# A mixer and a 32-expert layer on one core: 1536 weight columns pass through PSUM, and the loads of the second and third expert pair are cut anew

## Chip, cores, metric

One core of a Trainium2 chip. The metric is the time of one execution on the device in microseconds (us); lower is better.

## What is computed

One layer on 256 frames of width 1024, all in float32. Three mixers (retention, sliding-window attention, attention to a memory) share one input projection and one output projection; then comes a mixture of experts, 4 of 32 for each frame:

```python
h = rms_norm(x, g_mix[l])
proj = h @ w_in[l]
...
logits = (ht @ w_router + b_router).astype(jnp.float32)
top_val, top_idx = lax.top_k(logits, TOP_K)
gates = jax.nn.softmax(top_val, axis=-1)
...
hu = xb @ w_up[e] + b_up[e]
x_glu, x_lin = jnp.split(hu, 2, axis=-1)
x_glu = jnp.minimum(x_glu, SWIGLU_LIMIT)
x_lin = jnp.clip(x_lin, -SWIGLU_LIMIT, SWIGLU_LIMIT)
act = x_glu * jax.nn.sigmoid(SWIGLU_ALPHA * x_glu) * (x_lin + 1.0)
y = act @ w_down[e] + b_down[e]
```

The up projection of an expert is 1024 x 2048, the down projection 1024 x 1024. All 32 experts are read from memory, whatever is chosen.

## The kernel before

The experts go in 16 pairs (numbered 0 to 15), and each expert takes up to 64 frames at a time; the two of a pair stand side by side in the columns of TensorE. The weights of a pair are cut into 12 chunks of 128 x 4096 values (2 MB): eight for the up projection (numbered 0 to 7; 0 to 3 make the first half of the hidden columns, 4 to 7 the second) and four for the down projection (8 to 11). They go into a ring of 12 slots, so that chunk j of a pair takes slot j, once TensorE has used chunk j of the pair before.

SyncE (SP) issues nearly all loads, in order, and waits on counters ahead of each: `slot_used` is raised by TensorE when it is through with a chunk, `half_used` when it has used a part of one. During the mixers (up to about 130 us) SP brings in pair 0 (`first_chunk`, L437, and the pieces of L467 and L472), each as a slot comes free of mixer data. Pair 1 comes with `second_pair` (L484): its chunks stand in `FIRST_ORDER`, the order in which pair 0 uses them (0, 1, 4, 5, 2, 3, 6 to 11), and chunk 0 comes in quarters, chunks 1 to 5 in halves (L497). Pair 2's chunk 0 comes in three pieces (L507), its chunks 1 to 5 and pair 3's 0 to 5 one by one (L515), the rest of both by twos (L518). Pairs 4 to 11 come in transfers of four chunks (L525), pairs 12 and 13 by twos, pair 14 mostly by twos (L530 to L541), pair 15 by ones and at the end by halves (L545). TensorE learns of landings by `two_in[d]`, which counts the transfers for chunks 2d and 2d+1, and `odd_in`; `TWO_LOADS` says how many are due (`wait_chunk`, L1460).

On TensorE a pair is (`pair`, L1502): gather the frames of the pair with 16 products of `xy` and the selection `sel` (L1400), two `combine`s of the pair before (L1439), four biases (L1390), eight up chunks (L1543), turns of the activations (L1137), four down chunks (L1595), with two more combines before the end. VectorE scales what is gathered into `XT` (L817), clamps and multiplies (L1102 to L1110) and builds `sel` for the next pair; ScalarE does the sigmoids and copies results out of PSUM (L769 to L790).

Between mixers and experts stands a chain of small steps for each of two row tiles t: the router (`route`), its root of squares (`square_half` on ScalarE, L750, then GpSimd, L614 to L619), `choose` (L1002) which finds the four largest, `count` (L1346) which numbers the frames of each expert, `place_and_select` (L1027) which builds the first `sel`, and `gather_first` (L1405). TensorE's first chunk of pair 0 (L1543) waits for the first scaled columns, `xt_first`. The second half of pair 0's chunk 0 is kept in `early_half` and used after chunk 2 (L1568).

## Time and profile before

| | us |
|---|---|
| median of 3 runs | 1029.41 (1028.43 to 1029.58) |
| the profiled execution | 1030.23 |
| its span, first to last instruction | 1028.2 |
| TensorE busy (matmul) | 982.9, 96% |
| VectorE busy | 202.6, 20% |
| ScalarE busy | 115.6, 11% |
| DMA | 425.06 MB, 413 GB/s on average |

All times of the trace count from the first instruction of the profiled execution. Busy TensorE isn't TensorE at its peak: matmuls overlap, and their ends are modelled. A matmul in float32 with 512 columns stands as two records. The share of a DMA row is the mean over the core's sixteen DMA engines. "us to landing" is the time from the issue of a transfer to the moment when all of it has landed.

### The profile page before, as it was taken

How to read it: one execution, taken by the hardware profiler on the slowest of the kernel's cores; microseconds unless marked ns; L12 is line 12 of the kernel's file. 1: busy time of each engine (PE TensorE's matmuls, PEld its weight loads, DVE VectorE, ACT ScalarE, POOL GpSimd, SP SyncE). 2: the span in 40 equal slices, each digit the busy share in tenths (PEclk: the TensorE clock that was granted, in tenths of full speed). 3: DMA queues.
4: the chain of work that ended last, by engine and by line, in shares of the span. 5: the costliest groups of instructions: out<-in, count | busy, mean ns of one | idle time of the engine just before them, and what ended most of it. 6: DMA issues, size and time to landing. Idle time of an engine off the chain costs nothing.

```text
span 1028.2 us, 10912 instructions
## 1 busy us (share of the span) xinstructions
PE 982.9 (96%) x4512; PEld 395.4 (38%) x4512; DVE 202.6 (20%) x486; ACT 115.6 (11%) x246; POOL 12.8 (1%) x26
## 2 busy tenths in 40 slices
PE   9999999999999999799898989999898999999998
PEld 5446553434343434243332424343242434332432
DVE  0456132121212121211121111111121121211112
ACT  2427101010101010000000000000000010100000
POOL 0200000000000000000000000000000000000000
PEclk9999999999999999999998999999999999999999
DMA  9985899999999999999999999999999999999996
GB/s 361 413 369 218 324 348 428 422 434 432 422 438 440 433 431 439 433 431 441 431 431 431 434 420 429 426 437 439 428 436 418 435 431 432 428 433 426 429 424 281
DMA packets 22472, 425.06 MB, mean 413 GB/s; under 512 B 3856, under 2 KB 4624, under 8 KB 7472
## 3 DMA queue, kind: packets, MB, share of 16 engines
q1 hardware_dynamic: 22064, 424.17, 97.2%
q10 hardware_dynamic: 384, 0.54, 0.2%
q8 instruction: 18, 0.29, 0.1%
q14 instruction: 6, 0.05, 0.0%
HBM read 423.65 MB, written 1.05 MB: 413 GB/s over the span
## 4 chain that ended last, share of the span: by engine, by line
PE 58%; DMA 40%; SPq 1%; DVE 0%; issue 0%; ACT 0%; POOLq 0%; POOL 0%; DVEq 0%
DMA everything<-in_w_moe 39%; PE psum L1595 20%; PE psum L1543 17%; PE psum L1175 4%; PE psum L1439 4%; PE psum L1308 3%; PE psum L1137 2%; PE psum L1400 2%; PE psum L1150 1%; PE psum L1167 1%; SPq L561 1%; PE psum L1390 1%; PE psum L1492 1%; PE psum L1158 1%; DMA everything<-in_x_turned 0%; PE psum L1448 0%
## 5 line engine op out<-in xcount | busy, mean ns | idle before, releaser
L1543 PE MATMUL psum<-everything 128*64 128x512 f32 x2040 | 448.4, 596 | 6.8 <-DMA everything<-in_w_moe 6.6
L1543 PEld LDWEIGHTS psum<-everything 128*64 128x64 f32 x2040 | 143.3, 137 | 296.3 <-issue 281.7
L1595 PE MATMUL psum<-everything 128*64 128x512 f32 x960 | 226.8, 621 | 31.8 <-DMA everything<-in_w_moe 31.8
L1595 PEld LDWEIGHTS psum<-everything 128*64 128x64 f32 x960 | 69.9, 142 | 174.6 <-issue 171.8
L1102 DVE TENSOR_SCALAR everything<-psum 128x512 f32<-128x512 f32 x32 | 22.1, 692 | 389.4 <-PE psum L1543 389.4
L817 DVE TENSOR_TENSOR everything<-psum,everything 128x512 f32<-128x512 f32 (+1 forms) x38 | 25.0, 663 | 325.9 <-PE psum L1400 310.4
L1439 PE MATMUL psum<-everything 128*128 128x512 f32 x126 | 61.0, 605 | 0.0
L1400 PEld LDWEIGHTS psum<-everything 128*128 128x128 f32 x480 | 54.7, 192 | 12.2 <-issue 12.2
L769 ACT ACTIVATE everything<-everything 128x512 f32<-128x512 f32 x32 | 20.2, 631 | 346.3 <-DVE everything L1102 346.3
L1400 PE MATMUL psum<-everything 128*128 128x128 f32 x480 | 57.6, 278 | 0.0
L1175 PE MATMUL psum<-everything 128*128 128x512 f32 x96 | 42.1, 594 | 0.0
L790 ACT ACTIVATE everything<-psum 128x256 f32<-128x256 f32 (+1 forms) x48 | 20.1, 454 | 189.6 <-PE psum L1595 175.7
L1137 PEld LDWEIGHTS psum<-everything 128*128 128x128 f32 x236 | 25.5, 141 | 31.9 <-issue 29.3
L1137 PE MATMUL psum<-everything 128*128 128x128 f32 x236 | 34.7, 281 | 0.7 <-DVE everything L1110 0.5
L1439 PEld LDWEIGHTS psum<-everything 128*128 128x128 f32 x126 | 21.4, 189 | 27.9 <-issue 27.9
L778 ACT ACTIVATE everything<-psum 128x512 f32<-128x512 f32 x32 | 19.1, 598 | 98.6 <-PE psum L1137 97.8
L1308 PE MATMUL psum<-everything 128*128 128x512 f32 x64 | 28.9, 596 | 0.0
L1175 PEld LDWEIGHTS psum<-everything 128*128 128x128 f32 x96 | 18.0, 190 | 22.2 <-issue 22.2
L772 ACT ACTIVATE everything<-psum 128x256 f32<-128x256 f32 x16 | 6.2, 385 | 166.0 <-PE psum L1137 166.0
L1104 DVE TENSOR_SCALAR everything<-psum 128x512 f32<-128x512 f32 x32 | 22.1, 692 | 5.3 <-PE psum L1543 5.3
L1110 DVE TENSOR_TENSOR everything<-everything 128x512 f32<-128x512 f32 x32 | 22.2, 693 | 1.1
L1106 DVE SCALAR_TENSOR_TENSOR everything<-everything 128x512 f32<-128x512 f32 x32 | 22.2, 693 | 1.1
(168 smaller groups left out, 334.3 us busy)
## 6 DMA issues: line engine op xcount, KB each, us to landing
everything<-in_w_moe SPq DMA_DIRECT2D x22, 4096.0 KB, 38.5
everything<-in_w_moe SPq DMA_DIRECT2D x38, 2048.0 KB, 17.4
everything<-in_w_moe SPq DMA_DIRECT2D x24, 1024.0 KB, 9.4
everything<-in_w_in SPq DMA_DIRECT2D x3, 2048.0 KB, 24.3
everything<-in_w_out SPq DMA_DIRECT2D x2, 2048.0 KB, 11.3
everything<-in_w_moe SPq DMA_DIRECT2D x8, 512.0 KB, 5.8
everything<-in_w_mem_kv SPq DMA_DIRECT2D x1, 2048.0 KB, 16.9
everything<-in_w_in SPq DMA_DIRECT2D x1, 1024.0 KB, 8.6
```

What stands on the lines that cost most here:

```text
L817: return V.tensor_tensor(dst, src.rearrange("p (k n) -> p k n", k=kn), g, ALU.mult)
L1102: V.tensor_scalar(glu, psum[:, i], LIMIT, None, ALU.min).then_inc(glu_ready, 1)
L1104: V.tensor_scalar(lin, psum[:, 2 + i], LIMIT, -LIMIT, ALU.min, ALU.max).then_inc(up_read, 1)
L1106: V.scalar_tensor_tensor(out=lin, in0=lin, scalar=1.0, in1=glu, op0=ALU.add, op1=ALU.mult).then_inc(lin1_ready, 1)
L1110: V.tensor_tensor(sig, lin, sig, ALU.mult).then_inc(act_ready, 1)
L1137: return pe.transpose(dst, src, ident[0:n, 0:n])
L1175: mm = pe.matmul(psum[:, b], hT[:, k, t * P:(t + 1) * P], w_group_sb[n][:, k], start=k == 0, stop=k == KD - 1)
L1308: mm = pe.matmul(psum[:, MIXED_BANKS[c]], catT[:, k, t * P:(t + 1) * P], w_out_sb[n][:, k], start=i == 0, stop=i == KD - 1)
L1400: mm = pe.matmul(psum[:, banks[k // 4], c:c + P], xy[:, t, k * P:(k + 1) * P], sel[:, t], start=t == 0, stop=t == TILES - 1)
L1439: pe.matmul(psum[:, RESULT_BANKS[c]], back[:, t], Y[:, n * N:(n + 1) * N], start=start, stop=False, skip_group_check=True).then_inc(combin ...
L1543: mm = pe.matmul(psum[r:r + SLOTS, bank], XT[:, k, r:r + SLOTS], weights[i][:, column:column + N], start=first and k == 0 and j >= half, s ...
L1595: mm = pe.matmul(psum[r:r + SLOTS, DOWN_BANKS[n]], actT[:, 2 * i + k, r:r + SLOTS], slot[:, column:column + N], start=i == 0 and k == 0, s ...
```

## The change

- Once both tiles have been routed and chosen, ScalarE copies the first 1536 columns of pair 0's chunk 9 (the tenth) from slot 9 into the PSUM banks 6, 7 and 5. SP then loads the first 1536 columns of pair 1's chunk 4 (the fifth) into that place of slot 9. When TensorE has used three chunks of pair 0, so that slot 4 is free, ScalarE copies the 1536 columns from PSUM into slot 4. Pair 0 reads them there in its down projection, and pair 1 reads its chunk 4 partly from slot 9. The missing 1536 columns of pair 1's chunk 9 are loaded behind pair 2's chunk 4.
- Pair 1's chunk 0 comes in quarters and chunk 1 in halves, as before; chunks 2, 3 and 5 now come whole, chunks 4 and 9 as 2560 columns. Pair 2's chunk 0 comes whole. In pair 14 the chunks 8 and 9 come one by one.
- The first gather is split: the columns of chunk 0 first, then those of chunk 1, and the one that only `early_half` needs inside pair 0. The gathers' PSUM banks change, the product that counts all frames moves behind pair 0's chunk 4, and the selection compares with the count itself.
- The squares of the last tile are summed in two halves on ScalarE, and GpSimd adds them.
- Pair 1 gathers four of eight blocks, adds two biases, and does the rest of gathers, combines and biases before its third chunk. Pair 14 gathers for pair 15 between its down chunks and leaves two combines to pair 15, which does all four before its third chunk. In all other pairs two biases stand ahead of the wait for the scaled columns.
- Three counters become one (`heads_read`), with the same waits.

The diff, cut to its core:

```diff
-    ROUTE_BANKS = (2, 5)
-    FIRST_GATHER_BANKS, GATHER_BANKS = (6, 7), (1, 3)
+    ROUTE_BANKS, COUNT_BANKS = (2, 5), (2, 4)
+    FIRST_ROWS = (0,), (2, 3)
+    FIRST_GATHER_BANKS, GATHER_BANKS = (1, 4, 3, 3, 4, 4, 4, 4), (3, 1)
...
-    SECOND_PIECES = {0: (0, 1, 2), **{j: (0, 2, 4) for j in range(1, 6)}}
-    THIRD_PIECES = (0, 1, 2, 4)
+    MOVED, MOVED_FROM, MOVED_TO, MOVED_BANKS = 3 * 512, 9, 4, (6, 7, 5)
+    SECOND_PIECES = {0: (0, 2, 4), 1: (0, 4, 8), MOVED_TO: (3, 8), MOVED_FROM: (3, 8)}
     LATE_SLOT = 10
     LATE_PIECES = ((2048, 4096), (0, 1024), (1024, 2048))
     TWO_LOADS = [int(sum(1 + (len(LATE_PIECES) - 1 if j == LATE_SLOT else j == LATE_SLOT + 1) + (len(SECOND_PIECES[j]) - 1 if j in SECOND_PIECES else 1)
-                         for j in (2 * d, 2 * d + 1))) for d in range(TWOS)]
+                         for j in (2 * d, 2 * d + 1))) + (d in (MOVED_TO // 2, MOVED_FROM // 2)) for d in range(TWOS)]
...
+            sp.wait_ge(moved, len(MOVED_BANKS))
+            sp.dma_start(slots[MOVED_FROM][:, 0:MOVED], chunk(PAIR_CHUNKS + MOVED_TO)[:, 0:MOVED]
+                         ).then_inc(two_in[MOVED_TO // 2], 16)
+
...
-                    pieces = SECOND_PIECES.get(j, (0, 4))
+                    pieces = SECOND_PIECES.get(j, (0, 8))
                     for c0, c1 in zip(pieces, pieces[1:]):
-                        if c1 == pieces[-1] == 2:
+                        if c1 == pieces[-1]:
                             wait_used(1, place)
-                        elif c1 < 4:
+                        else:
                             halves += 1
                             sp.wait_ge(half_used, halves)
-                        else:
-                            wait_used(1, place)
-                        part = slice(c0 * SLOT_COLS // 4, c1 * SLOT_COLS // 4)
+                        part = slice(c0 * SLOT_COLS // 8, c1 * SLOT_COLS // 8)
                         sp.dma_start(slots[j][:, part], chunk(PAIR_CHUNKS + j)[:, part]).then_inc(two_in[j // 2], 16)
                 for d in range(TWOS):
                     credit(d)
-                for c0, c1 in zip(THIRD_PIECES, THIRD_PIECES[1:]):
-                    if c1 < 4:
-                        halves += 1
-                        sp.wait_ge(half_used, halves)
-                    else:
-                        wait_used(2, 0)
-                    part = slice(c0 * SLOT_COLS // 4, c1 * SLOT_COLS // 4)
-                    sp.dma_start(slots[0][:, part], chunk(2 * PAIR_CHUNKS)[:, part]).then_inc(two_in[0], 16)
-
-            def pair(q, p, single=0, begun=(0, 0, 0)):
+
+            def pair(q, p, single=0, rest=False):
                 for d in range(TWOS):
                     if d < single:
                         for i, done in enumerate((two_in[d], odd_in[d])):
-                            if i >= begun[d]:
-                                wait_used(q, 2 * d + i)
-                                sp.dma_start(slots[2 * d + i], chunk(q * PAIR_CHUNKS + 2 * d + i)).then_inc(done, 16)
+                            wait_used(q, 2 * d + i)
+                            sp.dma_start(slots[2 * d + i], chunk(q * PAIR_CHUNKS + 2 * d + i)).then_inc(done, 16)
+                            if rest and 2 * d + i == MOVED_TO:
+                                sp.dma_start(slots[MOVED_FROM][:, 0:MOVED], chunk(PAIR_CHUNKS + MOVED_FROM)[:, 0:MOVED]
+                                             ).then_inc(two_in[MOVED_FROM // 2], 16)
...
-                for d in range(1, TWOS - 1):
+                for d in range(1, TWOS - 2):
                     wait_used(q, 2 * d + 1)
                     sp.dma_start(two_slots[d], two_of_pair(q, d)).then_inc(two_in[d], 16)
                     credit(d)
-                for j, done in ((PAIR_CHUNKS - 2, two_in[TWOS - 1]), (PAIR_CHUNKS - 1, quarters_in[0])):
+                for j, done in zip(range(UP_CHUNKS, PAIR_CHUNKS), (two_in[4], odd_in[4], two_in[5], quarters_in[0])):
                     wait_used(q, j)
                     sp.dma_start(slots[j], chunk(q * PAIR_CHUNKS + j)).then_inc(done, 16)
...
-            pair(2, 2, single=3, begun=(1, 0, 0))
+            pair(2, 2, single=3, rest=True)
...
+            act.wait_ge(two_in[MOVED_FROM // 2], 32)
+            act.wait_ge(routed, TILES)
+            act.wait_ge(chosen_ready, TILES)
+            for i, b in enumerate(MOVED_BANKS):
+                nc.scalar.activation(psum[:, b], slots[MOVED_FROM][:, i * N:(i + 1) * N], ACT.Copy).then_inc(moved, 1)
+            act.wait_ge(moved, len(MOVED_BANKS))
+            act.wait_ge(slot_used, MIX_CHUNKS + 3)
+            for i, b in enumerate(MOVED_BANKS):
+                nc.scalar.activation(slots[MOVED_TO][:, i * N:(i + 1) * N], psum[:, b], ACT.Copy).then_inc(moved, 1)
...
 
-            def gather_first(t, ks):
+            def gather_first(t, ks, done=None):
 
...
                 if t == 1:
-                    mm.then_inc(gathered, 1)
-
-            gather_first(0, range(KD // 2))
+                    mm.then_inc(done, 1)
+
+            for ks in FIRST_ROWS:
+                gather_first(0, ks)
             count(1)
             pe.wait_ge(expert_biases_in, 16 * 4)
             pe.wait_ge(whose_ready, 1)
             bias(0, (0, 2), start=True)
-            gather_first(1, range(KD // 2))
-            pe.matmul(psum[:, 4, 256:256 + E], ones, chosen[:, 0], start=True, stop=False)
-            pe.matmul(psum[:, 4, 256:256 + E], ones, chosen[:, 1], start=False, stop=True).then_inc(counted, 1)
+            for ks, done in zip(FIRST_ROWS, (gathered_part, gathered_part)):
+                gather_first(1, ks, done)
+
+            def count_all():
+
+                pe.wait_ge(xt_first, 2)
+                pe.matmul(psum[:, 4, 256:256 + E], ones, chosen[:, 0], start=True, stop=False)
+                pe.matmul(psum[:, 4, 256:256 + E], ones, chosen[:, 1], start=False, stop=True).then_inc(counted, 1)
 
             def turn_gates():
 
...
                     if j % 2 == 0:
                         pe.wait_ge(two_in[j // 2], 16 * (len(LATE_PIECES) + 2) if j == LATE_SLOT else 32)
                 elif j % 2 == 0:
-                    pieces = 0 if j or second else len(THIRD_PIECES) - 2
-                    pe.wait_ge(two_in[j // 2], q * 16 + 16 * (TWO_LOADS[j // 2] - 1 + pieces))
+                    pe.wait_ge(two_in[j // 2], q * 16 + 16 * (TWO_LOADS[j // 2] - 1))
...
+                    at_once = not second and not last_one
+                    if not last_one:
+                        pe.wait_ge(up_read, 2 * q)
+                        gather(q, range(KD if at_once else KD // 2))
                     pe.wait_ge(y_ready, 2 * q)
-                    if not own:
-                        combine(q - 1, (2, 3), start=second)
-                    pe.wait_ge(xt_ready, 2 * q + 2)
+                    if at_once and not own:
+                        combine(q - 1, (2, 3))
                     pe.wait_ge(whose_ready, q + 1)
-                    bias(p, range(4), start=True).then_inc(biased, 1)
+                    bias(p, (0, 2), start=True)
+                    pe.wait_ge(xt_ready, 2 * q + (2 if at_once else 1))
+                    if at_once:
+                        bias(p, (1, 3), start=True).then_inc(biased, 1)
                 for place, j in enumerate(order):
+                    if j == 2 and (second or last_one):
+                        if second:
+                            gather(q, range(KD // 2, KD))
+                        combine(q - 1, (2, 3) if second else range(4), start=second)
+                        pe.wait_ge(xt_ready, 2 * q + 2)
+                        bias(p, (1, 3), start=True).then_inc(biased, 1)
...
                                 column = (2 * part + e) * N
+                                rows = weights[i]
+                                if second and j == MOVED_TO and i == 0 and column < MOVED:
+                                    rows = slots[MOVED_FROM]
                                 mm = pe.matmul(psum[r:r + SLOTS, bank], XT[:, k, r:r + SLOTS],
-                                               weights[i][:, column:column + N],
+                                               rows[:, column:column + N],
                                                start=first and k == 0 and j >= half,
                                                stop=k == KD - 1, skip_group_check=True)
...
+                        if first and i == 0 and j == 1:
                             mm.then_inc(half_used, 1)
                         if first and i == 0 and j == half + 1:
+                            pe.wait_ge(count_ready, 1)
                             gather_first(0, range(KD // 2, KD))
-                            gather_first(1, range(KD // 2, KD))
+                            gather_first(1, range(KD // 2, KD), gathered)
+                        elif first and i == 0 and j == 1:
+                            gather_first(0, (1,))
+                            gather_first(1, (1,), gathered)
+                        elif first and i == 0 and j == half:
+                            count_all()
                         elif first and i == 0 and j == 2:
                             turn_gates()
...
+                        pe.wait_ge(xt_first, 2)
...
+                    if next_too and i == 1:
+                        pe.wait_ge(up_read, 2 * q + 2)
+                        gather(q + 1, range(KD // 2))
+                    elif next_too and i == 2:
+                        gather(q + 1, range(KD // 2, KD))
...
+                    if first and UP_CHUNKS + i == MOVED_FROM:
+                        pe.wait_ge(moved, 2 * len(MOVED_BANKS))
...
-                            if last and (n, k) == (1, 1):
+                            if last and (n, k) == (1, 1) and not next_too:
...
+                                moved_here = first and UP_CHUNKS + i == MOVED_FROM and column < MOVED
+                                rows = slots[MOVED_TO] if moved_here else slot
                                 mm = pe.matmul(psum[r:r + SLOTS, DOWN_BANKS[n]], actT[:, 2 * i + k, r:r + SLOTS],
-                                               slot[:, column:column + N],
+                                               rows[:, column:column + N],
...
-            with pe.Fori(BDOWN_PAIR + 1, PAIRS - 1) as q:
+            with pe.Fori(BDOWN_PAIR + 1, PAIRS - 2) as q:
                 pair(q, q)
+            pair(PAIRS - 2, PAIRS - 2, next_too=True)
```

`rs_chosen` (VectorE) holds `chosen` times the root for the first two experts, made in `choose`; the first `sel` compares `iota` with the count in PSUM and multiplies by it.

SP's queue from the last loads of pair 0 on, before (w_moe are the expert weights, everything is the one buffer that holds slots and the rest):

```order
L472 DMA everything<-in_w_moe 128x2048 [waits routed]
L497 DMA everything<-in_w_moe 128x1024 [waits half_used]
L497 DMA everything<-in_w_moe 128x1024 [waits slot_used]
L497 DMA everything<-in_w_moe 128x2048 [waits half_used]
L497 DMA everything<-in_w_moe 128x2048 [waits slot_used]
L497 DMA everything<-in_w_moe 128x4096 [waits slot_used] x6
L507 DMA everything<-in_w_moe 128x1024 [waits half_used] x2
L507 DMA everything<-in_w_moe 128x2048 [waits slot_used]
L515 DMA everything<-in_w_moe 128x4096 [waits slot_used] x5
L518 DMA everything<-in_w_moe 128x8192 [waits slot_used] x3
```

and with the change:

```order
L475 DMA everything<-in_w_moe 128x2048 [waits routed]
L478 DMA everything<-in_w_moe 128x1536 [waits moved]
L502 DMA everything<-in_w_moe 128x1024 [waits half_used]
L502 DMA everything<-in_w_moe 128x1024 [waits slot_used]
L502 DMA everything<-in_w_moe 128x2048 [waits half_used]
L502 DMA everything<-in_w_moe 128x2048 [waits slot_used]
L502 DMA everything<-in_w_moe 128x2560 [waits slot_used]
L502 DMA everything<-in_w_moe 128x4096 [waits slot_used] x6
L502 DMA everything<-in_w_moe 128x2560 [waits slot_used]
L502 DMA everything<-in_w_moe 128x4096 [waits slot_used] x2
L511 DMA everything<-in_w_moe 128x4096 [waits slot_used] x5
L513 DMA everything<-in_w_moe 128x1536
```

The load of 1536 columns stands ahead of all of pair 1's, five pairs of halves have become one (the two rows of halves before stand for chunks 1 to 5), and the missing columns of chunk 9 stand behind five loads of pair 2.

TensorE from the second count to the first chunk of pair 0, before (L1411 gathers, L1422 and L1423 count all frames, L1543 is the up projection):

```order
L1350 MATMUL psum<-everything 128x32 [waits chosen_ready]
L1352 MATMUL psum<-everything 128x32
L1390 MATMUL psum<-everything 128x512 [waits whose_ready,expert_biases_in]
L1390 MATMUL psum<-everything 128x512
L1411 MATMUL psum<-everything 128x128 [waits sel_ready]
L1411 MATMUL psum<-everything 128x128 x3
L1422 MATMUL psum<-everything 128x32
L1423 MATMUL psum<-everything 128x32
L1543 MATMUL psum<-everything 64x512 [waits two_in0,xt_first]
```

and with the change (L1430 gathers, L1580 is the up projection):

```order
L1370 MATMUL psum<-everything 128x32
L1372 MATMUL psum<-everything 128x32 [waits chosen_ready]
L1409 MATMUL psum<-everything 128x512 [waits whose_ready,expert_biases_in]
L1409 MATMUL psum<-everything 128x512
L1430 MATMUL psum<-everything 128x128 [waits sel_ready] x2
L1430 MATMUL psum<-everything 128x128
L1580 MATMUL psum<-everything 64x512 [waits two_in0,xt_first]
L1580 MATMUL psum<-everything 64x512 x3
L1580 MATMUL psum<-everything 64x512 [waits xt_ready]
L1580 MATMUL psum<-everything 64x512 x3
L1430 MATMUL psum<-everything 128x128 [waits sel_first]
L1430 MATMUL psum<-everything 128x128 [waits sel_ready]
```

One product of the count now stands ahead of its wait, one gather and the two counting products have left the place before the first chunk, and a gather of either tile stands behind the second chunk's first half.

## Rows read from the trace of the kernel before

**Rows 1.** The page, part 2: what the DMA engines moved, in 40 slices of the span.
```profile
GB/s 361 413 369 218 324 348 428 422 434 432 422 438 440 433 431 439 433 431 441 431 431 431 434 420 429 426 437 439 428 436 418 435 431 432 428 433 426 429 424 281
```
**Rows 2.** The chain of waits in order of time: start us, us, what.
```profile
394.46 40.82 DMA everything<-in_w_moe
435.28 0.14 issue
...
493.33 0.14 issue
```
**Rows 3.** Windows about the first dry point: last columns PEclk, DMA share, GB/s.
```profile
140.00:142.00 2.00, 2.00 (x12) 0.71 (x10) 0.00 (x0) 0.00 (x0) 0.00 (x0) 1.00 0.64 143
...
140.50:141.00 0.50, 0.50 (x6) 0.21 (x4) 0.00 (x0) 0.00 (x0) 0.00 (x0) 1.00 0.78 90
```
**Rows 4.** SP's issues (start us, us) and behind each its DMA row (us to landing).
```profile
132.00 0.43 SPq L472 DMA_DIRECT2D everything<-in_w_moe  x1
everything<-in_w_moe SPq DMA_DIRECT2D x1, 1024.0 KB, 7.6
...
134.18 0.33 SPq L472 DMA_DIRECT2D everything<-in_w_moe  x1
everything<-in_w_moe SPq DMA_DIRECT2D x1, 1024.0 KB, 8.9
...
139.85 0.33 SPq L497 DMA_DIRECT2D everything<-in_w_moe  x1
everything<-in_w_moe SPq DMA_DIRECT2D x1, 512.0 KB, 4.4
```
**Rows 5.** Timeline before the first chunk: start us, us, engine, line, operation.
```profile
135.89 0.19 ACT L759 ACTIVATION_READ_ACCUMULATOR everything<-everything 128x1 f32 x1
...
136.79 0.50 DVE L1079 TENSOR_SCALAR everything<-everything 128x64 f32<-128x64 f32 x4
...
138.73 0.65 PE L1543 MATMUL psum<-everything 128*64 128x512 f32 x2
```
**Rows 6.** Groups of ScalarE: xcount | busy us, mean ns | idle before.
```profile
L769 ACT ACTIVATE everything<-everything 128x512 f32<-128x512 f32 x32 | 20.2, 631 | 346.3 <-DVE everything L1102 346.3
```
**Rows 7.** SP's issues of pair 1's chunks 4 and 5, second halves, and a landing.
```profile
147.58 0.33 SPq L497 DMA_DIRECT2D everything<-in_w_moe  x1
everything<-in_w_moe SPq DMA_DIRECT2D x1, 1024.0 KB, 8.7
...
153.14 0.33 SPq L497 DMA_DIRECT2D everything<-in_w_moe  x1
```
**Rows 8.** Pair 2's chunk 4: issue and landing; TensorE's timeline at pair 1's chunk 8.
```profile
211.50 0.33 SPq L515 DMA_DIRECT2D everything<-in_w_moe  x1
everything<-in_w_moe SPq DMA_DIRECT2D x1, 2048.0 KB, 15.1
...
222.54 0.60 PE L1595 MATMUL psum<-everything 128*64 128x512 f32 x2
```
**Rows 9.** TensorE behind three waits (idle before in brackets), and a window (clock, share, GB/s).
```profile
435.42 5.97 PE L1595 MATMUL psum<-everything 128*64 128x512 f32 x16 [4.53 <-DMA everything<-in_w_moe]
...
436.00:438.00 2.00, 2.00 (x7) 0.54 (x5) 0.00 (x0) 0.00 (x0) 0.00 (x0) 0.50 1.14 492
...
493.47 5.35 PE L1595 MATMUL psum<-everything 128*64 128x512 f32 x16 [3.85 <-DMA everything<-in_w_moe]
...
669.41 3.65 PE L1595 MATMUL psum<-everything 128*64 128x512 f32 x16 [2.48 <-DMA everything<-in_w_moe]
```
**Rows 10.** The last two-chunk load before pair 4's first load, and that one's issue.
```profile
290.96 0.33 SPq L518 DMA_DIRECT2D everything<-in_w_moe  x1
everything<-in_w_moe SPq DMA_DIRECT2D x1, 4096.0 KB, 28.2
...
312.42 0.35 SPq L525 DMA_DIRECT2D everything<-in_w_moe  x1
```
**Rows 11.** TensorE's timeline in pair 15: the last release by a transfer.
```profile
1013.18 1.94 PE L1492 MATMUL psum<-everything 128*64 128x512 f32 x8 [0.54 <-DMA everything<-in_w_moe]
```

111 lines of the change are left out of this document (60 added, 51 removed).

## The prediction

> **What bounds the kernel now.** I read the page first: two numbers stand out, TensorE's busy share (table above) and the DMA stream, which from the seventh slice on never falls below 418 GB/s, but for the last slice [rows 1]. Then the chain of waits in order of time: up to 394 us it is TensorE work without a break, later a weight transfer, some matmuls, the next transfer, and so on [rows 2]. A pair costs the stream 58.05 us (from the release at 435.28 to that at 493.33, three transfers of four chunks, so 4.84 us for a chunk and 2.42 for half of one) [rows 2]. TensorE needs less for a pair: it starts behind the stream and has caught it at 394 us. From then on TensorE can only follow it. The end follows it too: at 1013.18 us a transfer releases TensorE, and what comes behind is fixed [rows 11]. So a microsecond counts only if the stream gains or loses it, and there on the one of its sixteen engines that is last.
>
> That last point decides much. A transfer is spread over sixteen DMA engines and has landed when the slowest is through. At 140 to 142 us the mean share of the engines is 0.64 [rows 3]: a hole of 2 x 0.36 = 0.7 us per engine. Yet the transfer issued at 134.18 lands 8.9 us later, at 143.1, and the next one, issued at 139.85, at 144.3 [rows 4]. For 512 KB at some 425 GB/s 1.2 us are due, and 1.2 us lie between the two landings. The last engine never waited; the others did.
>
> **The moved columns.** ScalarE ends its second set of exponentials at 136.1 and was free then [rows 5]. Three copies of 128x512 follow. An activation of that shape between buffers takes 631 ns [rows 6]; into PSUM no row shows one, so half of that to twice that; I take 0.63, the nearest shape. They end at 138.0, the 768 KB transfer is issued at 138.1 and has data on the engines about 1.0 us later (an issue at 139.85 shows as a share of 0.78 at 140.5 to 141 [rows 3, 4]), at 139.1, before the hole. It fills the hole: mean engine +0.7 us, last engine nothing, since its queue was full. What it could gain is the 143.1 itself: the landing before came at 132.00 + 7.6 = 139.6, so this megabyte took 3.5 us where 2.4 is usual [rows 2, 4]. Gain 0 to 1.1 us; I take 0.3. At twice the price per copy the issue would be at 140.0, still before the last engine is dry.
>
> **TensorE before the first chunk.** The second count now ends with the `before` product, the selection is built without a step before it, one block of columns is gathered instead of four, and the two counting products stand behind the start. VectorE however must still do the four placing operations (0.50 us) and the gate weights before the first block, so the start moves from 138.73 by about 1 us [rows 5]. The deferred block (two gathers) and the count, together about 0.8 us, then come inside the first pair. By the fourth chunk in order TensorE is 0.1 us ahead of before: nothing. The copies back (three on ScalarE, behind the third chunk in order) end near 149 us, long before TensorE comes to the tenth chunk.
>
> **Whole chunks.** Half of pair 1's sixth chunk was issued when TensorE was half through with that slot; now all of it goes at 153.1, with the old second half [rows 7]. (The fifth, cut to 2560 columns, waits for its slot in the same way.) The queue by then holds the same columns as before, of which the last landed at 147.58 + 8.7 = 156.3; new data are there at 154.1. Again others idle, by 1 to 2 us, and the last one does not. Larger transfers may be quicker per column: the 14 chunks that landed from 156.3 to 226.6 [rows 7, 8], four of them cut, took 5.02 us each, the uncut 4.84. If cutting made all of that excess, the four uncut now would gain 2.5 us; if other things did, nothing. The cut ones can't be told apart in these sums, and ten of the 14 are whole already, so I take 0.3, and give back 0.2 for the cut tenth chunk and the two more single loads of pair 14. Net 0.1.
>
> A rule speaks here, in sentences that the sum does not use: the Trainium skill (DMA: Bandwidth & Descriptors, section "Anatomy of one DMA — SWDGE (gpsimd) path") gives every DMA about 2.0 us besides its bytes. By it three transfers fewer would be an estimated 6 us less if the price were paid in the stream; it says itself that it is mostly the latency of completion.
>
> **Pair 1.** TensorE gathers half, adds two biases and starts its first chunk some 4 us earlier; it does the other half of the gathers, two combines and two biases behind the second chunk. Pair 2's first two chunks are thus issued 4 us earlier into a queue that isn't dry (15.1 us lie between the issue at 211.50 and its landing [rows 8]), and the later ones where they were. Nothing gained or lost.
>
> **The new wait.** The 1536 columns of pair 1's tenth chunk are issued behind pair 2's fifth chunk, and the semaphore of chunks nine and ten counts them already at chunk nine. Pair 2's fifth chunk landed at 211.50 + 15.1 = 226.6 [rows 8]. With 768 KB less ahead of it and 768 KB behind it, the rest lands again at 226.6, less my gains: 226.2. TensorE stands before chunk nine at 222.5 [rows 8]. It waits 3.7 us. After waits of 3.85 and 4.53 us at the same line sixteen matmuls take 5.35 and 5.97 us; after 2.48 us they take 3.65 [rows 9]. The granted clock is 0.50 behind the longest, that is 1.2 instead of 2.4 GHz [rows 9]. So 1.6 us more: TensorE is 5.3 us late. Behind it are the slots, so every load of SP from the seventh chunk of pair 2 on is issued 5.3 us later. The tightest is the first four-chunk load: issued at 312.42, while the one before it, issued at 290.96, lands at 319.2 [rows 10]. It would have data at 312.4 + 5.3 + 1.0 = 318.7. The last engine is due at 318.8 with the gains: it just isn't dry, others idle 3 us. Restarting in a row costs something, as the 143.1 above: 0 to 1 us, I take 0.4. From there on the slack grows, since TensorE gains on the stream in every pair until 394.
>
> **The end.** Pair 15's gathers move into pair 14, two combines the other way; TensorE has as much to do in both pairs together as before, and still waits for a transfer, by 0.54 us, at the tail [rows 11], which covers the reshuffle. If that cover were gone, the excess would count one to one. The tail is unchanged.
>
> **Sum.** -0.3 (hole) -0.1 (pieces) +0.4 (restart at 319) = 0.0 us against the profiled execution's own 1030.23 us (span 1028.2 and 2.0 around it), which is 0.8 above the median of 1029.41. Against that median I forecast **1029.4 us**, and for this case alone 1028.2 to 1030.8.
>
> **Rivals.**
>
> *The stream's gain counts in full.* If the hole, not the last engine, sets the position: 0.7 for the hole, 1.1 for the slow megabyte, 0.3 for whole chunks, and some 0.4 if the lagging engine catches up in the second gap, 2.5 us: 1026.9. For it: the 3.5 us are right at the dry point. Against: the landings at 143.1 and 144.3, and the new gap at 153 takes more than 1 us back from the mean engine. Chance 0.12.
>
> *A price per transfer in the stream.* The 512 KB issued at 139.85 take 4.4 us to land, 3.2 more than their bytes [rows 4]. Paid once for each of three transfers fewer: 9.6 us less, 1019.8. The 1.2 us between the landings at 143.1 and 144.3 refute it. Chance 0.01.
>
> *The new wait reaches the stream.* TensorE's wait at chunk nine holds back the load of 312.42; it decides from a delay of 319.2 - 312.4 - 1.0 = 5.8 us on, one to one. A wait of 4.9 us with the clock's 2.5 (the row of 4.53 gives 2.3) is 7.4: +1.6, and a restart of 1.0: +2.6 us, 1032.0. For it: all numbers stand at the edge. Against: the landing must be 1 us later than worked out. Chance 0.18.
>
> *The transfer of moved columns is late* (copies queued behind something on ScalarE): the hole stays, and SP, which issues in order, holds back pair 1's first loads. From an issue after 142 us on the last engine is dry: each microsecond counts, 1030.4 for 143. Chance 0.04; its time lies within the forecast's range.
>
> **How the numbers follow.** The forecast has 0.65. Range 1027.4 to 1031.7: the forecast's own, widened by 0.8 us toward the first rival and by 0.9 toward the third, so that about 0.1 is left out on either side. What a measurement of this kernel tells from no change is about 0.2%, 2.1 us: faster by more 0.13, within 0.70, slower by more 0.17.
>
> **What would show it.** Right: data share near 1 at 140 to 142, a gap at 153 to 154, a wait of L1648 (the down projection, L1595 now) near 222.5 us of 3 to 4.5 us with the clock at 0.50 behind it, a drop in share near 317, and the last release by a transfer within 1 us of 1013.2. Wrong: no wait at 222, a rest that lands before it, or a share below 1 anywhere after 330.

## The result, and the profile after

The changed kernel is slower. Five runs of each gave a median of 1033.14 us (1032.53 to 1034.9) against 1029.14 us (1028.43 to 1029.58), a ratio of 1.0042 (95% interval 1.0031 to 1.0053): about 4 us, outside the range of the prediction. The profiled execution took 1032.91 us, its span is 1031.0 (before: 1030.23 and 1028.2), so 2.7 to 2.8 us of the 4 can be looked for in these traces. 0.6 of that is there already at 134 us: SP's issue of 134.18 [rows 4] stands at 134.75 here. The other profiles scatter by as much (133.5 to 134.5), and that load lands no later than before (134.75 + 8.1 = 142.9, before 143.1).

Stretches of the changed kernel (busy time and count of PE, PEld, DVE, ACT, POOL; granted clock; DMA share; GB/s):

```profile
140.00:142.00 2.00, 2.00 (x11) 0.61 (x8) 0.00 (x0) 0.00 (x0) 0.00 (x0) 1.00 0.96 368
153.00:154.00 1.00, 1.00 (x8) 0.35 (x6) 1.00 (x6) 0.00 (x0) 0.00 (x0) 1.00 0.80 328
154.00:155.00 1.00, 1.00 (x8) 0.37 (x6) 0.75 (x4) 0.00 (x0) 0.00 (x0) 1.00 0.42 170
228.00:230.00 2.00, 1.81 (x6) 0.66 (x8) 0.00 (x0) 0.00 (x0) 0.00 (x0) 0.50 1.01 434
232.00:233.00 1.00, 1.00 (x6) 0.15 (x2) 0.00 (x0) 0.00 (x0) 0.00 (x0) 1.00 0.31 131
340.00:900.00 560.00, 531.37 (x2493) 201.20 (x2489) 89.94 (x190) 40.38 (x79) 0.00 (x0) 0.98 1.00 432
```

The hole at 140 to 142 us is filled: share 0.96 for the 0.64 of [rows 3]. New gaps stand at 153 to 155 and at 232. From 340 us on nothing is missing. TensorE of the changed kernel:

```profile
138.23 3.65 PE L1580 MATMUL psum<-everything 128*64 128x512 f32 x16
...
228.19 4.98 PE L1648 MATMUL psum<-everything 128*64 128x512 f32 x16 [3.09 <-DMA everything<-in_w_moe]
...
1016.15 1.94 PE L1516 MATMUL psum<-everything 128*64 128x512 f32 x8 [0.54 <-DMA everything<-in_w_moe]
```

The second row is the new wait, 3.09 us, with the clock at 0.50 (1.2 GHz) behind it. The last answers to [rows 11]: the same release with the same 0.54 us of waiting, 2.97 us later. So what was lost was lost early and is kept to the end. The chain of waits of the changed kernel says where TensorE hands over to a transfer; the kernel before had only TensorE in it up to 394 us [rows 2]:

```profile
203.40 10.47 PE psum L1580 x48
...
214.65 13.41 DMA everything<-in_w_moe
...
228.19 4.98 PE psum L1648 x16
```

The transfer is the owed rest of pair 1's chunk 9, landed at 228.06. Two more views give each load's issue (start, duration) and, in the row of the DMA view for the same moment, the time from issue to landing. First SP's issues in the changed kernel (pair 1's chunks 4, 5, 2 and 3; pair 2's chunks 1 and 2; chunks 6 and 7 together; the first four-chunk load):

```profile
148.58 0.33 SPq L502 DMA_DIRECT2D everything<-in_w_moe  x1
154.15 0.33 SPq L502 DMA_DIRECT2D everything<-in_w_moe  x1
158.06 0.33 SPq L502 DMA_DIRECT2D everything<-in_w_moe  x1
164.05 0.33 SPq L502 DMA_DIRECT2D everything<-in_w_moe  x1
...
198.68 0.33 SPq L511 DMA_DIRECT2D everything<-in_w_moe  x1
207.02 0.33 SPq L511 DMA_DIRECT2D everything<-in_w_moe  x1
...
230.16 0.33 SPq L517 DMA_DIRECT2D everything<-in_w_moe  x1
...
319.44 0.35 SPq L524 DMA_DIRECT2D everything<-in_w_moe  x1
```

and the landings of five of them (148.58, 164.05, 207.02, 230.16, 319.44):

```profile
everything<-in_w_moe SPq DMA_DIRECT2D x1, 1280.0 KB, 8.1
...
everything<-in_w_moe SPq DMA_DIRECT2D x1, 2048.0 KB, 9.1
...
everything<-in_w_moe SPq DMA_DIRECT2D x1, 2048.0 KB, 9.2
...
everything<-in_w_moe SPq DMA_DIRECT2D x1, 4096.0 KB, 14.3
...
everything<-in_w_moe SPq DMA_DIRECT2D x1, 22.3
```

In the kernel before, the issues of pair 2's chunk 2 and of its chunks 6 and 7 are

```profile
204.63 0.33 SPq L515 DMA_DIRECT2D everything<-in_w_moe  x1
...
223.59 0.33 SPq L518 DMA_DIRECT2D everything<-in_w_moe  x1
```

and they land 12.2 and 17.6 us after their issue. Pair 2's loads thus go out 2.4 and 6.6 us later than before. I call **lead** the time from a load's issue to the landing of the load ahead of it, and **interval** the time between the two landings; a full queue gives 4.9 us for a chunk that is loaded by itself (4.8 to 4.9 in the table further down) and 9.7 for two (4.84 each, [rows 2]). All of these are good to 0.1 us, as the rows of the DMA view are. Chunk 5 has a lead of 148.6 + 8.1 - 154.15 = 2.5 us, and the three chunks 5, 2 and 3 land in 173.15 - 156.68 = 16.5 us where 14.7 are due (in halves, before, they took 15.2). Chunks 6 and 7 have a lead of 2.8 us (the load ahead lands at 232.9) and an interval of 11.5 us, 1.8 too many. The four-chunk load has a lead of 2.9 us (the load ahead lands at 322.4) and loses nothing. One more load is late: pair 1's chunk 7, issued at 172.93 with a lead of 5.1 us, lands 5.7 us behind chunk 6 (183.7 and 178.0), 0.8 too many; before, these two landed 4.9 apart.

### The profile page after: what moved, and what is told of

Read it like the earlier page. It is cut to its first block, busy times and chain, and to the rows that moved or that the text cites. A ratio compares the mean times of both kernels' runs of the same rounds, so it can differ in the third digit from the quotient of the medians.

```text
span 1031.0 us, 10906 instructions
## 1 busy us (share of the span) xinstructions
PE 986.7 (96%) x4512; PEld 396.4 (38%) x4512; DVE 203.1 (20%) x487; ACT 118.8 (12%) x254; POOL 12.9 (1%) x27
## 4 chain that ended last, share of the span: by engine, by line
PE 57%; DMA 41%; SPq 1%; DVE 0%; issue 0%; ACT 0%; DVEq 0%
DMA everything<-in_w_moe 40%; PE psum L1648 20%; PE psum L1580 16%; PE psum L1195 4%; PE psum L1464 3%; PE psum L1328 3%; PE psum L1419 2%; PE psum L1157 2%; PE psum L1187 1%; DMA everything<-in_w_in 1%; PE psum L1409 1%; PE psum L1516 1%; PE psum L1170 1%; PE psum L1178 1%; SPq L560 1%; PE psum L1473 0%
## 5 line engine op out<-in xcount | busy, mean ns | idle before, releaser
L1580 PE MATMUL psum<-everything 128*64 128x512 f32 x2040 | 447.1, 594 | 5.4 <-DMA everything<-in_w_moe 5.3
L1580 PEld LDWEIGHTS psum<-everything 128*64 128x64 f32 x2040 | 142.8, 137 | 292.4 <-issue 279.2
L832 DVE TENSOR_TENSOR everything<-psum,everything 128x512 f32<-128x512 f32 (+2 forms) x39 | 25.3, 650 | 324.0 <-PE psum L1419 311.9
## 6 DMA issues: line engine op xcount, KB each, us to landing
everything<-in_w_moe SPq DMA_DIRECT2D x43, 2048.0 KB, 15.2
```

The lines of the kernel that those rows point to most:

```text
L832: return V.tensor_tensor(dst, src.rearrange("p (k n) -> p k n", k=kn), g, ALU.mult)
L1580: mm = pe.matmul(psum[r:r + SLOTS, bank], XT[:, k, r:r + SLOTS], rows[:, column:column + N], start=first and k == 0 and j >= half, stop=k ...
```

## The experiments

A line per kernel: the median, and what it is over the kernel before on the same chip (medians), with the interval of the ratio. One ratio is good to about 1 us, a difference of two to about 1.3. Each experiment has 11 runs, e1 six.

| kernel | us | over before | ratio, 95% |
|---|---|---|---|
| changed | 1033.14 | +4.0 | 1.0031-1.0053 |
| e1 halves | 1033.10 | +3.7 | 1.0019-1.0043 |
| e2 rest at ten | 1031.82 | +2.5 | 1.0014-1.0032 |
| e4 both | 1031.71 | +2.3 | 1.0010-1.0028 |
| e7 e4, pair 1 as before | 1031.74 | +2.1 | 1.0015-1.0033 |
| e9 e7, whole chunks | 1031.85 | +2.2 | 1.0011-1.0029 |
| e10 e7, third pieces | 1031.08 | +1.8 | 1.0008-1.0026 |
| e13 e10, 512 columns | 1030.90 | +1.6 | 1.0004-1.0022 |
| e11 e4, no moved columns | 1029.99 | +0.7 | 0.9996-1.0014 |
| e14 e4, cut | 1029.97 | +0.7 | 0.9997-1.0015 |
| e15 e11, cut | 1029.11 | -0.1 | 0.9992-1.0010 |
| e16 e4, no rest | 1029.68 | +0.4 | 0.9993-1.0012 |
| before + wait (e6) | 1030.68 | +1.3 | 1.0006-1.0024 |
| before + whole (e5) | 1030.93 | +1.2 | 0.9999-1.0017 |
| before + pair 1 (e8) | 1029.55 | -0.1 | 0.9987-1.0005 |
| before + 0.9 us of TensorE (e12) | 1029.71 | +0.4 | 0.9999-1.0017 |

**Is it the wait, the whole chunks, or both?** e1 loads chunks 5, 2 and 3 in halves again:

```diff
-    SECOND_PIECES = {0: (0, 2, 4), 1: (0, 4, 8), MOVED_TO: (3, 8), MOVED_FROM: (3, 8)}
+    SECOND_PIECES = {0: (0, 2, 4), **{j: (0, 4, 8) for j in (1, 5, 2, 3)}, MOVED_TO: (3, 8), MOVED_FROM: (3, 8)}
```

> The changed kernel, but pair 1's chunks 5, 2 and 3 come in halves again, the first half as soon as TensorE is through with the slot's first half. Theory A (two dry points: the DMA queue runs out near 153 us because chunk 5 is issued whole, and again near 231 us because TensorE waits before pair 1's chunk 8; landings fell behind by 1.4 us at the first and 1.8 us at the second): no low share at 154 us, time 1.2 to 1.8 us under the changed kernel, about 1031.6. Theory B (only the wait at chunk 8 costs; the last engine was never dry at 154): the same as the changed kernel, 1033.1. Theory C (the reshuffle of pairs 14 and 15 costs): 1033.1 too.

It gave nothing that can be told, though the gap is gone: e1 loses the time at three later loads instead, 2.2 us at pair 2's chunk 2 (table below), 1.0 at its chunks 6 and 7 (issued at 230.26, landed at 243.8, the load ahead at 233.0), and 1.4 at the first four-chunk load (issued at 321.19 with a lead of 0.9, landed at 342.9). The stretch of the old gap reads in e1

```profile
153.00:156.00 3.00, 3.00 (x18) 0.83 (x16) 1.17 (x6) 0.38 (x2) 0.00 (x0) 1.00 1.02 393
```

e2 counts the owed rest on a semaphore that only chunk 9 waits for; e4 is e1 and e2 together:

```diff
-                                             ).then_inc(two_in[MOVED_FROM // 2], 16)
+                                             ).then_inc(odd_in[MOVED_FROM // 2], 16)
```

> The changed kernel, but the missing 1536 columns of pair 1's chunk 9 count on the counter that TensorE waits for ahead of chunk 9, not ahead of chunk 8. TensorE reaches chunk 9 near 229 us, the columns landed at 228.1. Theory A: the wait of 3.1 us and the slow clock behind it go, SP's next issues come 6 to 7 us earlier, the landing of pair 2's chunks 6 and 7 comes 1.8 us earlier: about 1031.3. Theory B: 2.8 to 4 us less, 1029.1 to 1030.3. Theory C: 1033.1.

> Both edits together. Theory A: 1.4 and 1.8 us add up, 1029.5 to 1030.2, the kernel before within 0.1%. Theory B: as the second edit alone. Theory C: 1033.1.

TensorE in e2 goes on where the changed kernel stood:

```profile
224.50 3.60 PE L1649 MATMUL psum<-everything 128*64 128x512 f32 x16
```

That takes 1.3 us off (1.6 against each one's own before), the halves on top 0.1. e6 is the other direction: the kernel before, with a wait for pair 2's chunk 4 put ahead of pair 1's chunk 8:

```diff
+                    if second and i == 0:
+                        pe.wait_ge(two_in[2], 16 * (TWO_LOADS[2] + 1))
                     wait_chunk(q, UP_CHUNKS + i, first)
```

> The kernel before, with one wait added: ahead of pair 1's chunk 8 TensorE waits until pair 2's chunk 4 has landed (226.6 us in the trace of before, 4.1 us later than TensorE comes there). Nothing else is changed. Theory A and B: a wait of 4 us, the clock at 0.50 behind it, the load of pair 2's chunks 6 and 7 issued 6 to 7 us later at 230 us and the queue dry: 1.5 to 2.5 us slower than before, about 1031. My prediction's own view (the last engine isn't dry, since its queue reaches to 231.5): no change, 1029.1. Theory C: 1029.1.

Alone in the old kernel the wait costs the same 1.3 us. The row of TensorE, and SP's issue of the four-chunk load:

```profile
225.94 5.35 PE L1597 MATMUL psum<-everything 128*64 128x512 f32 x16 [3.52 <-DMA everything<-in_w_moe]
```

```profile
296.10 0.33 SPq L518 DMA_DIRECT2D everything<-in_w_moe  x1
...
317.56 0.35 SPq L525 DMA_DIRECT2D everything<-in_w_moe  x1
```

The first of these lands 22.8 us after its issue, at 318.9, the second 22.0, at 339.6: a lead of 1.3 us, an interval of 20.7 for the 19.4 of four chunks (338.5 - 319.2 before, [rows 10]). Here the last engine had 1.3 us of work left when the load was issued, and 1.3 us were lost.

**Is the rest the new order of pair 1?** e7 is e4 with pair 1 in the order of before, e9 the same with whole chunks, e8 the kernel before with only the new order:

```diff
-                    at_once = not second and not last_one
+                    at_once = not last_one
...
-                        combine(q - 1, (2, 3))
+                        combine(q - 1, (2, 3), start=second)
...
-                    if j == 2 and (second or last_one):
-                        if second:
-                            gather(q, range(KD // 2, KD))
-                        combine(q - 1, (2, 3) if second else range(4), start=second)
+                    if j == 2 and last_one:
+                        combine(q - 1, range(4))
```

> The changed kernel with three things put right: chunks 5, 2 and 3 of the second load of a slot in halves again, the rest of chunk 9 counted on a semaphore that only chunk 9 waits for, and pair 1 (gather of all eight blocks, combine of pair 0's second half, four biases together, all ahead of its first chunk) in the order of the kernel before. The moved columns and the split of the last pairs stay. Theory R (the reordering of pair 1 delays the loads of pair 2's chunks 2 and 3 and lets the queue run dry near 208 us): about 1.9 us under the kernel with the first two put right (1031.7), 1029.3 to 1030.0, with the load of pair 2's chunk 2 issued within 0.5 us of 204.6 and the first four-chunk load landing within 1 us of 338.5. Theory M (the moved columns add traffic order or a start cost that stays): still 1031 or more, with the landing interval of pair 2's chunk 2 back under 5.5 us but the four-chunk load late by 1.5 us or more all the same. If the filled hole of 0.5 to 0.7 us is a gain that only the other losses hid: 1028.5 to 1029.2.

> As the one above, but chunks 5, 2 and 3 stay whole. If the gap at 153 to 155 us and the slow packets behind it are a loss that nothing later can absorb once pair 1 is in its old order: 1.0 to 1.6 us over the one above (1030.5 to 1031.5). If a later dry queue sets the landing of the four-chunk load in both, the two are within 0.3 us.

The core of e8, in the kernel before:

```diff
-                    gather(q)
+                    gather(q, range(KD // 2 if second else KD))
...
+                    if j == 2 and second:
+                        gather(q, range(KD // 2, KD))
+                        combine(q - 1, (2, 3), start=True)
+                        pe.wait_ge(xt_ready, 2 * q + 2)
+                        bias(p, (1, 3), start=True).then_inc(biased, 1)
```

> The kernel before with one thing alone: pair 1 gathers four blocks and adds two biases ahead of its first chunk, and gathers the other four, combines pair 0's second half and adds the other two biases behind its second chunk. Theory R: 1.3 to 2.0 us slower, 1030.7 to 1031.3, with the load of pair 2's chunk 2 issued 1.5 to 2.5 us later than 204.63 and the queue dry there. Rival (the prediction's: nothing gained or lost): within 0.3 us of the kernel before.

My theory fell. e8 costs nothing that can be told although its load of chunk 2 goes out at 206.41; e7 gains nothing that can be told over e4 (0.3 us by the medians), and e9 is within 0.1 of e7. e7 had lost the pieces of pair 2's chunk 0 as well, which the new order makes needless: that load goes out at 198.12 where before the first piece left at 195.19, and the stretch shows the hole:

```profile
196.00:200.00 4.00, 4.00 (x20) 1.29 (x18) 0.00 (x0) 0.00 (x0) 0.00 (x0) 1.00 0.74 258
```

e10 brings these pieces back, and still is at +1.8, inside the range of the rival that expected the deferred 768 KB to cost time somewhere. e5 is the kernel before with chunks 5, 2 and 3 whole; e12 does four gather products of pair 0 twice, which takes 0.9 us of TensorE in its trace (in this order: a line of e10, then e5, then e12):

```diff
+    THIRD_PIECES = (0, 2, 4, 8)
...
-    SECOND_PIECES = {0: (0, 1, 2), **{j: (0, 2, 4) for j in range(1, 6)}}
+    SECOND_PIECES = {0: (0, 1, 2), 1: (0, 2, 4), 4: (0, 2, 4)}
...
                             gather_first(0, range(KD // 2, KD))
+                            gather_first(0, range(KD // 2, KD))
```

> The changed kernel with four things put back: chunks 5, 2 and 3 in halves, the rest of chunk 9 on a semaphore of its own, pair 1 in the order of before, and pair 2's chunk 0 in its three pieces (the run with the first three left that chunk whole, was issued at 198.12 instead of 195.19, and its load took 7.48 us instead of 4.9). What is left of the change is the moved columns, the split first gather in pair 0 and the last pairs. Theory L (lead: each dry place adds its excess to the last engine, and nothing else matters): 2.0 to 2.6 us under 1031.7, so 1029.1 to 1029.8, with pair 2's first chunk issued near 195.0 and landed near 205, the rest of pair 1's chunk 9 near 226.3. Rival D (the deferred 768 KB cannot be loaded for nothing: with 768 KB less in the queue between 152 and 214 us it must run dry somewhere before the rest is issued, here at pair 1's chunk 7, issued at 172.3, and again at pair 2's first three chunks): 1030.5 to 1031.5, with about 1 to 1.5 us of excess in the intervals from 195 to 215.

> The kernel before with chunks 5, 2 and 3 of pair 1 loaded whole instead of in halves, and nothing else. Theory W (the gap at 153 to 155 us, in which 15 of 16 engines idle, costs a restart with slow first packets although the last engine was never dry): 0.8 to 1.6 us slower, 1030.2 to 1031.0. Rival (the prediction's: only the last engine counts): within 0.3 us, 1029.1 to 1029.7.

> The kernel before with 1.0 us more of TensorE's work in pair 0: the four second-half gather products of the first tile are done twice. All of pair 1's later loads are then issued 1.0 us later, as in the changed kernel they are 0.8 to 1.0 us later. If TensorE's pace in pair 0 counts (pair 1's chunk 7, issued at 171.9 when the first engine has 2.44 us of work left): 0.5 to 1.2 us slower, 1029.9 to 1030.6. If the lead of the stream covers it: within 0.2 us.

Neither e5 nor e12 is told from the kernel before (both intervals begin at 0.9999).

**Is it the moved columns?** e11 takes them out of the change (no copies, no extra load, chunks 1 to 5 in halves, chunk 9 whole); e13 moves 512 instead of 1536:

```diff
-    SECOND_PIECES = {0: (0, 2, 4), 1: (0, 4, 8), MOVED_TO: (3, 8), MOVED_FROM: (3, 8)}
+    SECOND_PIECES = {0: (0, 2, 4), **{j: (0, 4, 8) for j in range(1, 6)}}
...
-            sp.wait_ge(moved, len(MOVED_BANKS))
-            sp.dma_start(slots[MOVED_FROM][:, 0:MOVED], chunk(PAIR_CHUNKS + MOVED_TO)[:, 0:MOVED]
-                         ).then_inc(two_in[MOVED_TO // 2], 16)
...
-    MOVED, MOVED_FROM, MOVED_TO, MOVED_BANKS = 3 * 512, 9, 4, (6, 7, 5)
+    MOVED, MOVED_FROM, MOVED_TO, MOVED_BANKS = 512, 9, 4, (6,)
```

> The changed kernel without the moved columns: no copies on ScalarE, chunk 4 of pair 1 in halves and chunk 9 whole and in place, chunks 5, 2 and 3 in halves too; pair 1 in its new order, pair 2's chunk 0 whole, the split first gather and the last pairs as in the change. It differs from the run with two things put right (1031.7) by the moved columns alone. Theory D (the moved columns shorten the lead, so the queue runs dry later): 1029.0 to 1029.9, with the landing interval of pair 2's chunk 2, issued near 206.8, at 4.9 us instead of 6.3. Rival (the moved columns are worth what they fill, and the loss is elsewhere): 1032 or more.

> As the run with four things put back, but 512 columns (256 KB, 0.6 us of the stream) are moved instead of 1536. Theory D (what is moved comes off the lead and is paid at the rest's load; only what the hole at 140 us holds is won): faster than the run with 1536 columns by 0.5 to 1.2 us, and near the kernel before, 1028.6 to 1029.8. Theory L: equal to it or 0.3 us slower, since less of the hole is filled.

e11 is 1.7 us under e4 (good to 1.3) and no longer told from before: the part of the change that was to fill the hole costs some 1.7 us. e13 decides nothing (0.2 us under e10). Why the move costs is asked by the last three. In e14 and e15 pair 1 gathers two of eight blocks, so that TensorE is earlier (it computes with stale columns); in e16 the owed 768 KB are never loaded and pair 1 multiplies with what lies there:

```diff
-                        gather(q, range(KD if at_once else KD // 2))
+                        gather(q, range(KD if at_once else KD // 2) if not second else (3,))
...
-                            gather(q, range(KD // 2, KD))
+                            gather(q, (7,))
...
-                                sp.dma_start(slots[MOVED_FROM][:, 0:MOVED], chunk(PAIR_CHUNKS + MOVED_FROM)[:, 0:MOVED]
-                                             ).then_inc(odd_in[MOVED_FROM // 2], 16)
+                                sp.sem_inc(odd_in[MOVED_FROM // 2], 16)
```

> The changed kernel with halves and the rest of chunk 9 put right (1031.7 before), in which pair 1 gathers two blocks instead of eight: 12 products of 128x128, about 1.7 us of TensorE, are left out, so pair 1 computes with stale columns. The load of pair 2's chunk 2 is then issued about 1.7 us earlier, near 205.1, and the queue is not dry there. If dryness at that place is what the moved columns cost: 1.2 to 1.9 us faster, 1029.8 to 1030.5, with that load's landing interval near 4.9 instead of 6.3 us. If the moved columns cost something else, or the stream falls dry elsewhere instead: 1031.3 or more.

> The same 12 products left out of the changed kernel without the moved columns (1030.0 before), as the control. Its queue had 2.26 us left on the first engine at that place and was not dry, so the cut should give nothing: 1029.7 to 1030.1. If it becomes faster by as much as the one above, TensorE's time in pair 1 counts by itself and dryness is not the cause.

> The changed kernel with halves and the rest of chunk 9 put right (1031.7), in which the owed 768 KB of pair 1's chunk 9 are never loaded (pair 1 multiplies with what lies there). The stream has 1.87 us less to bring. If it is the bound from 230 us on, all of it is saved: 1029.6 to 1030.1. That would be only 0 to 0.4 us under the kernel without moved columns, which loads 768 KB more: the filled hole and 768 KB less together would then be worth next to nothing, because the queue between 150 and 215 us waits for TensorE's slots. If the filled hole is a gain that is kept: 1029.2 or less.

The clearest place is pair 2's chunk 2. In e4, and below it in e14, SP issues chunks 1 and 2 at

```profile
198.47 0.33 SPq L512 DMA_DIRECT2D everything<-in_w_moe  x1
...
206.81 0.33 SPq L512 DMA_DIRECT2D everything<-in_w_moe  x1
```

```profile
196.73 0.33 SPq L512 DMA_DIRECT2D everything<-in_w_moe  x1
...
203.74 0.33 SPq L512 DMA_DIRECT2D everything<-in_w_moe  x1
```

and they land after 11.2 and 9.2 us in e4, after 14.5 and 12.4 in e14. Read in the same way in all (us):

| kernel | chunk 1 lands | chunk 2 issued | lead | interval |
|---|---|---|---|---|
| before | 212.0 | 204.6 | 7.4 | 4.8 |
| e8 | 210.9 | 206.4 | 4.5 | 4.8 |
| e11 | 212.0 | 206.8 | 5.2 | 5.1 |
| e15 | 212.0 | 203.6 | 8.4 | 4.9 |
| changed | 211.3 | 207.0 | 4.3 | 4.9 |
| e2 | 212.1 | 206.6 | 5.6 | 5.0 |
| e14 | 211.2 | 203.7 | 7.5 | 4.9 |
| e4 | 209.7 | 206.8 | 2.9 | 6.3 |
| e1 | 209.3 | 206.4 | 2.9 | 7.1 |
| e16 | 209.2 | 206.5 | 2.8 | 7.1 |

At this load, where the lead is 2.9 us or less 1.4 to 2.2 us are lost; where it is 4.3 or more, 0.2 at most. (At other loads the rule has exceptions, given at the end.) Three kernels fall dry there (e1, e4, e16): those that owe 768 KB, which are then not in the queue, issue the load near 206.5, and have not already lost their time at 154 us. The last point is why the causes don't add up: the changed kernel and e2 lose at 154 what e1 and e4 lose at 208, and each pair ends within 0.3 us. The new order of pair 1, which issues chunk 2 some 2 us later, costs nothing that can be told while the queue is full (e8) and takes part in the loss where it isn't.

The sizes bear this out only in part. The cut gives e14 1.6 us (each against its own before) and the control e15, from which nothing was expected, 0.8. The 0.8 between them is what this dry place would be worth, less than the 1.3 us to which such a difference is good. With the cut the moved columns still cost 0.9.

Nor does e14's trace settle it. Its chunk 2 goes out earlier but lands at 216.1, as in e4 (216.0), because time was lost before, at pair 1's chunk 7:

```profile
172.13 0.33 SPq L502 DMA_DIRECT2D everything<-in_w_moe  x1
everything<-in_w_moe SPq DMA_DIRECT2D x1, 2048.0 KB, 11.6
```

Chunks 7, 8 and 9 land there in 16.1 us (from 175.6 to 191.7) where 12.9 are due; in e4 they took 13.9. This execution of e14 took 1031.33 us, 1.4 more than its median, so it may not stand for the others.

e16 saves 1.9 us, which is what 768 KB take (1536 of 4096 columns at 4.9 us a chunk: 1.84). This fits a stream that is the bound behind 230 us. But e16, which brings 1.8 us less than e11, is only 0.2 us under it: with the hole filled and the bytes gone, 1.6 us are idled away again. Of the differences of this last group only the 1.9 us of e16 are clear of their uncertainty. So are the price of the wait (e2, and e6 by itself) and, just so, that of the moved columns (e11 against e4), where the traces agree: the first four-chunk load lands at 340.5 in e4 and at 338.8 in e11.

## Why the prediction was wrong

**The frame held, its reach was wrong.** "A microsecond counts only if the stream gains or loses it" fits from 230 us on (e16; share 1.00 from 340). Between 150 and 215 us the stream has to wait at several loads for the slots that TensorE frees. A load can't be issued earlier because the stream is early, so what the stream gains at 140 it idles away at the next load whose slot isn't free.

**The moved columns.** Copies (below) and the filled hole came as said. The step that failed is the sum's -0.3: it priced the early 768 KB and not the later ones. When chunk 4 has landed the changed kernel and the one before have loaded the same bytes, and it lands at 156.7 here and at 156.3 before [rows 7] (156.1 in e4 and 155.7 in e11, whose last load of pair 0 goes out at the same 134.5). So nothing of the filled hole was left by then: chunk 4 was issued only at 148.58, when its slot was free, and its 2560 columns land 4.4 us behind the load ahead where 3.1 are due. From there until 214 us the queue is 1.8 us of work shorter than before, and the rest has to be paid in full at 228. No term of the sum and no rival held this. Measured: +1.7 us (e4 against e11). ScalarE in the changed kernel, three copies in 1.61 us, 0.54 each where I took 0.63:

```profile
136.34 1.61 ACT L771 ACTIVATE psum<-everything 128x512 f32<-128x512 f32 x3
```

**TensorE before the first chunk.** The start is early by 0.5 us in the trace, 1.1 if its late beginning is taken off, as predicted (1). But from the first chunk to the fourth it takes 152.17 - 138.23 = 13.9 us where 151.16 - 138.73 = 12.4 were, 1.5 more, not 0.8: the deferred gathers hold the next chunk up by 0.6 us (141.82 to 142.46), the count by 0.6 (146.04 to 146.60), and the three chunks, now broken up, take 0.3 more. The rows up to the fourth chunk in the changed kernel, then the fourth chunk in the kernel before:

```profile
141.82 0.71 PE L1430 MATMUL psum<-everything 128*128 128x128 f32 x4
142.46 3.65 PE L1580 MATMUL psum<-everything 128*64 128x512 f32 x16
146.04 0.41 PE L1447 MATMUL psum<-everything 128*128 128x32 f32 x2
...
146.60 3.65 PE L1580 MATMUL psum<-everything 128*64 128x512 f32 x16
...
152.17 3.22 PE L1580 MATMUL psum<-everything 128*64 128x512 f32 x14
```

```profile
151.16 3.65 PE L1543 MATMUL psum<-everything 128*64 128x512 f32 x16
```

"By the fourth chunk in order TensorE is 0.1 us ahead of before" should read 0.4 behind. e12 prices 0.9 us of such work at +0.4, not told from zero.

**Whole chunks.** The gap came where it was foretold, at 153 to 155. That "the last one does not" idle counted only who is dry, not how the restart goes: three chunks lost 1.8 us of landing time. In the change this was worth 0.0 to 0.1 us all the same, since without it the queue falls dry at 208 (e1, e4); alone, in e5, +1.2, which its interval doesn't tell from nothing.

**Pair 1.** "The later ones where they were" is wrong, 204.63 became 207.02. "Nothing gained or lost" is right by itself as far as e8 can tell, and wrong together with the owed columns.

**The new wait.** The mechanism, the place and the clock were right: 3.09 us for 3.7, clock 0.50, SP's issue 6.6 us later for 5.3. That the length of the wait came out is in part luck: TensorE stood there at 225.1 instead of 222.5, and the columns landed at 228.1 instead of 226.2, two misses that nearly cancel. Wrong was where the stream pays. I looked for the tightest load at 312 and didn't work out the one at 223.59, whose lead before was 231.5 - 223.6 = 7.9 us; my own 5.3 us of delay leave 2.6 of it. It shrank to 2.8 and cost 1.8. And where the four-chunk load was the tight one (e6), a lead of 1.3 us cost 1.3, not the 0.4 taken for a restart. Cost of the wait: 1.6 us taken out of the change (e2), 1.3 put into the kernel before (e6). The rival "the new wait reaches the stream" was of this kind and too small, since it had to carry the whole loss alone.

**The end.** Right: 0.54 us of waiting at the tail, no loss behind 340 us, so no cost of the reshuffle of pairs 14 and 15 shows.

Of the 4.0 us, 1.6 are the wait and 1.7 the moved columns with the dry queue that they leave. The other 0.7 (e11 over before) is within what can't be told from zero; the pair-0 work and pair 1's chunk 7 behind it are candidates (that load lands 0.8 us late in the changed kernel, 1.1 in e11, and not in the kernel before), and it stays open. So does where the moved columns lose the 0.9 us that the cut leaves. No version beat the kernel before.

## What to carry to other kernels

A transfer that is pulled forward into a hole is worth something only if the loads behind it can be issued earlier too; ask which slot each waits for, and work out the lead of every load behind the change, not of the tightest one in the old trace. Bytes that are deferred shorten the queue in the meantime and are paid in full where the stream is the bound. Losses at successive dry places don't add: mending one can expose the next, so test fixes together as well as singly.

## What the runs showed of the hardware

A queue can lose time before its last engine is idle. Loads issued 1.3, 2.8 and 2.9 us before the load ahead had landed lost 1.3 to 2.2 us (e6; the changed kernel and e16; e1 and e4). I had taken that lag as a cushion. But the four-chunk load of the changed kernel with a lead of 2.9 us lost none, so no threshold can be read from these runs.

Nor is a long interval by itself the sign of a dry queue. Pair 2's chunk 1 in e15 was issued 9.0 us before the load ahead of it landed (at 205.5), and its interval is 6.4 us, 1.5 too many:

```profile
196.55 0.33 SPq L506 DMA_DIRECT2D everything<-in_w_moe  x1
...
everything<-in_w_moe SPq DMA_DIRECT2D x1, 2048.0 KB, 15.4
```

The DMA share there, from 204 to 212 us, is 1.00. A transfer counts up its semaphore sixteen times, and in this trace fifteen of the counts of that load had come by 210.1 us, the last at 211.9: a single engine had fallen behind. Pair 2's chunks 6 and 7 in e16 (lead 5.6, interval 11.2 for 9.7) are another such case. What held these engines up no run shows. So an excess in one trace can be chance, and the causes above rest on the medians of many runs first and on the traces second.
